# One step of a hybrid decoder trunk on one core: the order of turning x, transposed sample columns, paired logits, a 528-column gather, and the order of the tail's back-turns

## The chip, the cores and the metric

The kernel runs on one core of a Trainium2 chip. Its time is the device time of one execution in microseconds; the median of three runs is given. Work of the core is done by TensorE (PE, with its weight loads shown apart as PEld), VectorE (DVE), ScalarE (ACT), GpSimd (POOL) and SyncE (SP, which here only issues transfers). Each has its own instruction queue, and the queues meet through semaphores.

## What is computed

One layer of a decoder trunk, for 256 prompt rows and 8 sample rows that share the weights (264 tokens, `TOK`), width 2048, all in fp32. Cut to its core:

```python
xn = rmsnorm(h, norm1_g)
c_val, c_gate, l_x, l_gate = split(xn @ w_in + b_in)         # 2048 -> 4 x 1024
c  = silu(layernorm(causal_dw_conv(c_val * sigmoid(c_gate), width 31)))
r  = rg_lru(causal_dw_conv(l_x, width 4)) * gelu(l_gate)     # recurrence over tokens
h  = h + concat(c, r) @ w_out
h  = h + hier_moe(rmsnorm(h, norm2_g))                       # below
h  = h + sigmoid(rmsnorm(h, ple_norm_g) @ w_pg + b_pg) * (p @ w_ple)
y  = rmsnorm(h, final_g)
# hier_moe: the group of 4 with the largest logit, the 2 best of its 8 experts,
#   out += (silu(x @ w_gate[e]) * (x @ w_up[e])) * combine[:, e] @ w_down[e]      (512 hidden)
```

All 32 experts' weights are read, 12.6 MB each.

## The kernel before

Activations lie transposed: `hT` and the like hold 128 channels on the partitions and the 264 tokens along the free axis, in 16 blocks (`KD = 16`). A turn brings a block from rows to columns or back through PE, with the identity `ident`; it has three parts, two of 128 tokens and one of the 8 sample tokens (`ROWS`). Every engine's stream is written out by hand, in the order in which it shall run; nothing is scheduled by a tool. The stages are:

1. **x turned.** x comes by two queues and SP. DVE and ACT sum the squares of the rows, ACT takes the root, DVE makes `rb` (the factor of each token). PE turns the 16 blocks of x (`turn_x`) into four PSUM banks in turn, and ACT copies them out as `hT`; block k waits for copy k-4. After eight blocks PE turns the vectors, then `rb`, then the other eight blocks. DVE scales into `xT`.
2. **w_in**: 32 products (`dense`, 16 chunks of 264 columns in two records each), with the convolution and the recurrence beside them on DVE. The last of the old rows are turned here.
3. **w_out**: 16 products (`split_product`): each weight tile is split into two fp32r parts, the high one by ACT, the rest by DVE (`rest_weights`), and three passes are added up. After product m come the router's logits of block m-1 (`logits`, 36 columns: 4 groups and 32 experts, all in bank 7) and the turn of block m-1 back to rows (`turn_rows`), which DVE and ACT take as `h_lo` and `h_hi`. In three places the tails of the states are turned (`turn_tails`, 8 turns each).
4. **Routing.** The logits and the sum of squares are copied by DVE into `lgT`, turned on PE, and DVE picks the groups, experts and places in `NSLOT` = 528 slots (two per token). Products of `w_ple` and the rank products fill PE meanwhile.
5. **Gather.** The chosen rows are brought to their slots by products with `onehot`, in two halves of `HX` = 296 columns, 80 products each and one for the scale; DVE takes them as `xTs`. The array has 64 further columns (`WIN`) so that a window of 64 slots can start anywhere (`XW` = 592).
6. **Experts.** For each of 32 experts PE multiplies a window of 64 slots with gate and up, then down, with the two column halves of the array in use at once, and spreads the result to the tokens; POOL copies the next window. Weights come by SP as pairs of 2.1 MB (`N_PAIR` = 192, six to an expert) into six pairs of ring slots. Pair g is issued when pair g-4 (for g under 8) or g-6 has been used; pairs 8 and 9 wait for the gather. Eight units (`UNITS`) of two blocks each add an expert's result to `hT` on DVE; behind the last expert their squares are summed there.
7. **Tail.** `w_pg`: 16 products, three plain (`PG_PLAIN`) and 13 split in two by ACT and DVE. Behind product 1 PE sums the squares over the partitions with `ones`; DVE makes `rb3` from it. For each tile DVE multiplies by `rb3`, ACT takes the sigmoid, DVE multiplies with `pleT` and adds to `hT`. The table `BACK` says behind which product PE turns which finished block back to rows, into three banks that are used again and again; DVE's `take_back` multiplies it by the final gain and frees the banks. Then the last scale and the output.

`slot_loaded` counts transfers, `acc_full` finished products, `h_added` finished blocks of `hT` in stage 3, `h3_ready` in the tail, `sq3_summed` the squares of the last units, `y_taken` the taken back-turns.

Of the kernel before, what the change touches and what calls it, by code (L numbers as in the profile page):

```python
# [17 lines left out]
TOK = SEQ + NB  # L18
# [14 lines left out]
NS = 13  # L33
NS_IN = 12
# [6 lines left out]
BACK = {4: (0,), 5: (1, 2), **{m: (m - 3,) for m in range(6, KD)}}  # L41
# [9 lines left out]
HX = XW // 2  # L51
# [57 lines left out]
def build(nc, a, o):  # L109
# [80 lines left out]
    rs_bc = place("rs_bc", [P, XW], F32, r_c + 4096)  # L190
    iota = place("iota", [P, XW], F32, r_c + 6464)
    onehot = place("onehot", [P, 3, XW], F32R, r_c + 8832)
# [84 lines left out]
    posn = rt("posn", [P, 3, E])  # L277
    pm1 = rt("pm1", [P, 1])
# [21 lines left out]
    hot_zero = sem("hot_zero")  # L300
    act_order = sem("act_order")
# [49 lines left out]
    lgT_ready = sem("lgT_ready")  # L351
    logits_turned = sem("logits_turned")
# [197 lines left out]
    def _(pool):  # L550
# [49 lines left out]
        for m in range(KD):  # L600
# [66 lines left out]
    def _(pe):  # L667
        def turn(out, src, r):

            if r == P:  # L670
                return pe.transpose(out, src, ident[:, :])  # L671
            return pe.matmul(out, src, ident[:, :], start=True, stop=True)  # L672
# [40 lines left out]
        pe.wait_ge(consts_ready, 5)  # L713
        for k in range(8):
# [159 lines left out]
        for m in range(KD):  # L874
# [29 lines left out]
        pe.wait_ge(lgT_ready, 1)  # L904
        for c in range(3):
            r = ROWS[c]
            src = lgT[0:65, c * P:c * P + r]
            if r == P:
# [963 lines left out]
```

## Time and profile before

| | |
|---|---|
| median of 3 runs | 1523.83 us (1523.17 to 1524.14) |
| profiled execution | 1522.83 us |
| its span, first to last instruction | 1521.0 us |
| PE busy (products) | 1445.9 us, 95% |
| PE weight loads | 826.3 us, 54% |
| DVE, ACT, POOL busy | 631.1, 232.5, 125.7 us |
| moved by the transfers | 482.63 MB, 317 GB/s over the span |
| mean granted clock of PE | 0.984 |

The profile is of one execution, and its places are in microseconds from the first instruction. Busy shares are over the whole span, and stages differ: one stage may wait for transfers and the next for PE. The end of a PE record is modelled, and a wide fp32 product of PE leaves two records in most of the views. The granted clock is a share of the full 2.4 GHz, so 0.50 is 1.2 GHz.

### The profile page before, as it was taken

To read this page: it belongs to the slowest core of one execution; us is meant where nothing else is said; L and a number is where in the kernel's file an instruction comes from. 1 tells how busy PE (TensorE), PEld (TensorE's weight loads), DVE (VectorE), ACT (ScalarE), POOL (GpSimd) and SP (SyncE) were. 2 spreads that over 40 slices of the span, in tenths; PEclk is the share of its full clock that TensorE was granted. 3 is DMA by queue.
4 is the path that set the end of the run, shared out by engine and by line. 5 is a ranking of instruction groups with operands and counts; after the bars stand their busy time and mean duration, and the time that the engine had idled before them with its cause. 6 is when DMAs were issued, how large, how long until landed. Compare 5 with 4: busy or idle time off the path is not lost.

```text
span 1521.0 us, 17860 instructions
## 1 busy us (share of the span) xinstructions
PE 1445.9 (95%) x7481; PEld 826.3 (54%) x7481; DVE 631.1 (41%) x1245; ACT 232.5 (15%) x384; POOL 125.7 (8%) x112
## 2 busy tenths in 40 slices
PE   6999999999999999999999999999999999999896
PEld 4888887888764334333333433343343334336795
DVE  3698844654452323322322322232232223226754
ACT  4000046633300000000000000000000000004432
POOL 1000002233000000000000000000000000000331
PEclk9999999999999999999999999999999999999998
DMA  9935340354459999999999999999999999996451
GB/s 285 286 138 193 140 111 1 91 144 139 194 239 377 427 427 428 427 427 429 427 427 427 428 428 429 427 426 427 427 427 429 427 428 427 427 420 182 126 162 62
DMA packets 122203, 482.63 MB, mean 317 GB/s; under 512 B 5242, under 2 KB 87714, under 8 KB 96611
## 3 DMA queue, kind: packets, MB, share of 16 engines
q1 hardware_dynamic: 120778, 475.45, 78.7%
q0 software_dynamic: 912, 2.89, 0.7%
q10 hardware_dynamic: 432, 3.15, 0.5%
q8 instruction: 60, 0.98, 0.3%
q14 instruction: 21, 0.16, 0.0%
HBM read 479.06 MB, written 3.42 MB: 317 GB/s over the span
## 4 chain that ended last, share of the span: by engine, by line
PE 66%; DMA 26%; ACT 3%; DVE 3%; issue 1%; SPq 0%; POOL 0%; DVEq 0%; ACTq 0%; POOLq 0%
DMA ring<-in_w_up_dram 25%; PE ps L1006 22%; PE ps L696 14%; PE ps L1028 7%; PE ps L970 4%; PE ps L804 3%; PE ps L806 3%; PE ps L805 3%; PE ps L1016 2%; PE ps L1099 1%; PE ps L672 1%; PE ps L710 1%; DVE sgl L1707 1%; PE ps L671 1%; PE ps L853 1%
## 5 line engine op out<-in xcount | busy, mean ns | idle before, releaser
L1006 PE MATMUL ps<-ring,xwin 128*64 128x512 f32 x1984 | 454.0, 599 | 22.6 <-DMA ring<-in_w_up_dram 22.5
L1723 DVE TENSOR_TENSOR hT<-hT,ps 128x528 f32<-128x528 f32 x256 | 171.7, 702 | 352.4 <-PE ps L970 349.1
L1006 PEld LDWEIGHTS ps<-ring,xwin 128*64 128x64 f32 x1984 | 140.4, 137 | 285.3 <-issue 285.3
L1028 PE MATMUL ps<-ring,hid 128*64 128x512 f32 x1024 | 238.2, 620 | 0.0
L696 PE MATMUL ps<-xT,ring 128*128 128x264 f32 x1024 | 231.2, 388 | 0.0
L696 PEld LDWEIGHTS ps<-xT,ring 128*128 128x128 f32 x1024 | 195.2, 191 | 33.5
L970 PE MATMUL ps<-sel,ysb 64*128 64x264 f32 x1024 | 185.0, 415 | 1.5 <-DVE ysb L1715 0.8
L970 PEld LDWEIGHTS ps<-sel,ysb 64*128 64x128 f32 x1024 | 103.5, 186 | 111.1 <-issue 100.6
L1028 PEld LDWEIGHTS ps<-ring,hid 128*64 128x64 f32 x1024 | 73.1, 142 | 148.8 <-issue 137.7
L642 POOL COPY xwin<-xTs 128x1024 f32 x31 | 32.4, 1047 | 840.1 <-PE ps L1006 820.3
L1276 ACT ACTIVATE sgl<-ps 64x512 f32<-64x512 f32 x32 | 18.9, 589 | 524.4 <-PE ps L1006 524.4
L1354 DVE SCALAR_TENSOR_TENSOR mix<-U,vT,mix 128x256 f32<-128x256 f32 x240 | 95.3, 477 | 0.0
L1715 DVE COPY ysb<-ps 128x512 f32<-128x512 f32 x32 | 22.1, 692 | 168.4 <-PE ps L1028 168.4
L1016 PE MATMUL ps<-ident,sgl 64*128 64x64 f32 x256 | 66.4, 399 | 10.7 <-DVE sgl L1707 10.7
L1494 DVE TENSOR_TENSOR ring_r<-ring,ring_r 128x2048 fp32r<-128x2048 f32 x29 | 66.3, 2290 | 24.5 <-ACT ring_r L1181 24.3
L1016 PEld LDWEIGHTS ps<-ident,sgl 64*128 64x128 f32 x256 | 62.0, 324 | 23.7 <-DVE sgl L1707 23.7
L1279 ACT ACTIVATE ysb<-ps 128x512 f32<-128x512 f32 x32 | 19.1, 598 | 355.4 <-PE ps L1028 355.4
L1707 DVE TENSOR_TENSOR sgl<-sgl,ps 64x512 f32<-64x512 f32 x32 | 22.1, 691 | 108.6 <-ACT sgl L1276 108.5
L1181 ACT ACTIVATE ring_r<-ring 128x2048 fp32r<-128x2048 f32 x29 | 55.3, 1908 | 52.4 <-DMA ring<-in_w_out_dram 43.2
L804 PE MATMUL ps<-gx_hi,ring_r 128*128 128x264 f32 x208 | 61.3, 295 | 0.0
L804 PE MATMUL ps<-x_hi,ring_r 128*128 128x264 f32 x208 | 60.6, 291 | 0.0
L806 PE MATMUL ps<-gx_hi,ring_r 128*128 128x264 f32 x208 | 59.7, 287 | 0.0
(338 smaller groups left out, 1278.3 us busy)
## 6 DMA issues: line engine op xcount, KB each, us to landing
ring<-in_w_gate_dram SPq DMA_DIRECT2D x64, 2048.0 KB, 16.0
ring<-in_w_up_dram SPq DMA_DIRECT2D x64, 2048.0 KB, 20.5
ring<-in_w_down_dram SPq DMA_DIRECT2D x64, 2048.0 KB, 18.2
ring<-in_w_in_dram SPq DMA_DIRECT2D x32, 512.0 KB, 8.8
ring<-in_w_in_dram SPq DMA_DIRECT2D x16, 1024.0 KB, 8.1
ring<-in_w_out_dram SPq DMA_DIRECT2D x16, 1024.0 KB, 5.9
ring<-in_w_pg_dram SPq DMA_DIRECT2D x16, 1024.0 KB, 5.9
ring<-in_w_ple_dram SPq DMA_DIRECT2D x2, 1024.0 KB, 4.9
```

Source lines behind the costliest of these rows:

```text
L696: mm = pe.matmul(ps[:, n % 3, 0:TOK], w, rhs[:, k, :], start=(k == 0), stop=(k == kt - 1))
L804: pe.matmul(out, w_hi, gate_hi(t)[:, k, :], start=(i == 0), stop=False)
L805: pe.matmul(out, w_hi, gate_lo(t)[:, k, :], start=False, stop=False)
L806: mm = pe.matmul(out, w_lo, gate_hi(t)[:, k, :], start=False, stop=(i == KD - 1))
L970: mm = pe.matmul(ps[:, 4 + 2 * (u % 2) + half, 0:TOK], ysb[rows, b, i * P:(i + 1) * P], sel[rows, :], start=True, stop=True)
L1006: mm = pe.matmul(ps[part * WIN:(part + 1) * WIN, 0, :], window(k), weights(2 * j + part)[:, kk * F:(kk + 1) * F], start=(k == 0), stop=(k ...
L1016: mm = pe.matmul(ps[:, 1, t * WIN:(t + 1) * WIN], sgl[WIN:2 * WIN, :].rearrange("w (p t) -> w t p", t=4)[:, t, :], ident[WIN:2 * WIN, WIN: ...
L1028: mm = pe.matmul(ps[half * WIN:(half + 1) * WIN, 2 + b, :], hid[:, t, :], weights(8 + t)[:, q * 512:(q + 1) * 512], start=(t == 0), stop=( ...
L1181: act.activation(ring_r[:, hi_slot(t), :, :].rearrange("p k c -> p (k c)"), ring[:, lo_slot(t), :], ACT.Copy).then_inc(w_hi_ready, 1)
L1354: return dve.scalar_tensor_tensor(out=out, in0=in0, scalar=s, in1=in1, op0=op0, op1=op1)
L1494: dve.tensor_tensor(lo, ring[:, lo_slot(t), :], hi.bitcast(F32), ALU.subtract).then_inc(w_lo_ready, 1)
L1723: dve.tensor_tensor(pair, pair, ps[:, b:b + 2, 0:TOK], ALU.add).then_inc(sems["added"], 1)
```

## The change

- **Start.** PE makes 36 transpositions of the identity into a bank that is free then (`WARM`), ahead of `turn_x`. ACT squares only the 8 sample rows, DVE both blocks of 128; ACT copies turned blocks as they come, and does its square behind the fourth, the root behind the sixth.
- **Turns.** The part with 8 sample tokens was a matmul with `ident`; it is now a transposition, as the others are.
- **Logits.** Two blocks at a time, behind every second product, the even one into partitions 0 to 35 of bank 7, the odd one into 64 to 99. The sum of squares goes to bank 5. ACT copies the even logits, DVE the odd ones and the squares. `fold`, a matrix made of two pieces of the identity, adds even and odd and turns them in one product; the squares are turned by a product with one column. That is six products for three.
- **Gather.** The halves have 264 columns, no more than the 528 slots; POOL clears the 64 spare columns of `xTs`.
- **Tail.** The sum of squares comes behind product 0. DVE makes `rbt` behind the eighth rest of the activations instead of the first. A tile's step on DVE is cut in two (`gate_in`, `gate_out`) with the rest of the weights between them, a tile earlier than before. Each back-turn comes one or two products later.

```diff
+WARM = 36
-BACK = {4: (0,), 5: (1, 2), **{m: (m - 3,) for m in range(6, KD)}}
+BACK = {**{m: (m - 5,) for m in range(5, 12)}, 12: (7, 8), 13: (9, 10), 14: (11,), 15: (12,)}
-HX = XW // 2
+HX = NSLOT // 2
...
         pool.wait_ge(logits_turned, 1)
+        pool.memset(xTs[:, :, NSLOT:], 0.0).then_inc(pad_zero, 1)
...
         def turn(out, src, r):
-            if r == P:
-                return pe.transpose(out, src, ident[:, :])
-            return pe.matmul(out, src, ident[:, :], start=True, stop=True)
+            return pe.transpose(out, src, ident[:, :])
...
         pe.wait_ge(consts_ready, 5)
+        for _ in range(WARM):
+            pe.transpose(ps[:, 7, 0:P], ident[:, :], ident[:, :])
         for k in range(8):
             turn_x(k)
...
-            pe.wait_ge(h_added, m + 1)
-            mm = pe.matmul(ps[0:NG + E, 7, 0:TOK], wr[:, m, :], hT[:, m, :], start=(m == 0), stop=(m == KD - 1),
-                           skip_group_check=True)
-            return mm
+            pe.wait_ge(h_added, m + 2)
+            for part in range(2):
+                pe.matmul(ps[part * 64:part * 64 + NG + E, 7, 0:TOK], wr[:, m + part, :], hT[:, m + part, :],
+                          start=(m == 0), stop=(m == KD - 2), skip_group_check=True)
...
+            if m >= 2 and m % 2 == 0:
+                logits(m - 2)
             if m >= 1:
-                logits(m - 1)
                 turn_rows(m - 1)
...
-        logits(KD - 1)
+        logits(KD - 2)
         pe.wait_ge(sq2_summed, KD)
-        pe.matmul(ps[64:65, 7, 0:TOK], ones[:, 0:1], acc2[:, :], start=True, stop=True, skip_group_check=True)\
-            .then_inc(logits_full, 1)
+        pe.matmul(ps[0:1, 5, 0:TOK], ones[:, 0:1], acc2[:, :], start=True, stop=True).then_inc(logits_full, 1)
...
-                last = pe.transpose(ps[:, 6, c * P:c * P + 65], src, ident[0:65, 0:65])
...
+            pe.matmul(ps[0:r, 6, c * P:c * P + NG + E], lgT[:, cols], fold[:, :], start=(c == 0), stop=True,
+                      skip_group_check=True)
+            mm = pe.matmul(ps[0:r, 6, c * P + 64:c * P + 65], sqh[0:1, 0, cols], ones[0:1, 0:1], start=False, stop=True,
+                           skip_group_check=True)
...
-            if m == 1:
+            if m == 0:
                 pe.wait_ge(sq3_summed, 2 * UNITS)
...
+        def take_x(first, n):
+            for k in range(first, first + n):
+                act.wait_ge(x_turned, k + 1)
+                act.activation(hT[:, k, :], ps[:, 3 + k % 4, 0:TOK], ACT.Copy).then_inc(hT_raw, 1)
+
+        take_x(0, 4)
         act.activation(xdump[0:NB, 1, :], xrow[0:NB, 2, :], ACT.Square, accum_out=ssum[0:NB, 2:3]).then_inc(ssq_act, 1)
-        act.activation(xdump[:, 1, :], xrow[:, 1, :], ACT.Square, accum_out=ssum[:, 1:2]).then_inc(ssq_act, 1)
+        take_x(4, 2)
...
+        take_x(6, KD - 6)
...
-        dve.wait_ge(ssq_act, 2)
+        dve.wait_ge(x_loaded[1], 16)
+        link(dve.tensor_tensor_reduce(xdump[:, 0, :], xrow[:, 1, :], xrow[:, 1, :], 1.0, 0.0, ALU.mult, ALU.add, ssum[:, 1:2]))
+        dve.wait_ge(ssq_act, 1)
...
-            if i == 0:
+            if i == 7:
                 dve.wait_ge(sum3_full, 1)
...
+        for m in range(4, KD):
+            gate_in(m)
+            if m + 3 < KD:
+                rest_weights(KD + m + 3)
+            gate_out(m)
             for b in BACK.get(m, ()):
                 take_back(b)
```

The start of ACT's stream, before; `hT<-ps` are the copies of turned blocks, `xdump<-xrow` the squares:

```order
L1135 DMA xrow<-in_x_prompt_dram 128x2048
L1138 ACT_TABLE_LOAD
L1138 ACTIVATE xdump,ssum<-xrow 8x2048
L1141 ACTIVATE xdump,ssum<-xrow 128x2048
L1143 ACT_TABLE_LOAD
L1143 ACTIVATE ssum<-ssum 128x3
L1146 ACTIVATE hT<-ps 128x264 x16
```

And of the change:

```order
L1141 DMA xrow<-in_x_prompt_dram 128x2048
L1143 ACT_TABLE_LOAD
L1143 ACTIVATE ssum<-ssum 128x1
L1148 ACTIVATE hT<-ps 128x264 x4
L1151 ACTIVATE xdump,ssum<-xrow 8x2048
L1148 ACTIVATE hT<-ps 128x264 x2
L1154 ACTIVATE ssum<-ssum 128x3
L1148 ACTIVATE hT<-ps 128x264 x10
```

The copies moved ahead of the squares and the root, the square of 128 rows left ACT, and the second table load is gone.

PE's stream behind the last `w_out` product, before (`36x264` are logits, `1x264` the sum of squares, `ident,hT` a turn back to rows, `ident,lgT` the turn of the logits):

```order
L671 MATMUL ps<-ident,hT 128x128 [waits rows_lo,rows_hi,h_added]
L671 MATMUL ps<-ident,hT 128x128
L672 MATMUL ps<-ident,hT 8x128
L853 MATMUL ps<-hT,wr 36x264 [waits h_added]
L900 MATMUL ps<-acc_89,ones 1x264 [waits sq2_summed]
L671 MATMUL ps<-ident,hT 128x128 [waits rows_lo,rows_hi,h_added]
L671 MATMUL ps<-ident,hT 128x128
L672 MATMUL ps<-ident,hT 8x128
L909 MATMUL ps<-ident,lgT 128x65 [waits lgT_ready]
L909 MATMUL ps<-ident,lgT 128x65
L911 MATMUL ps<-ident,lgT 8x65
```

And of the change:

```order
L860 MATMUL ps<-hT,wr 36x264 [waits h_added]
L860 MATMUL ps<-hT,wr 36x264
L907 MATMUL ps<-acc_89,ones 1x264 [waits sq2_summed]
L676 MATMUL ps<-ident,hT 128x128 [waits rows_lo,rows_hi,h_added]
L676 MATMUL ps<-ident,hT 128x128
L676 MATMUL ps<-ident,hT 8x128
L914 MATMUL ps<-fold,lgT 128x36 [waits lgT_ready]
L916 MATMUL ps<-ones,sqh 128x1
L914 MATMUL ps<-fold,lgT 128x36
L916 MATMUL ps<-ones,sqh 128x1
L914 MATMUL ps<-fold,lgT 8x36
L916 MATMUL ps<-ones,sqh 8x1
```

The two last blocks of logits stand behind each other now, and six products take the place of three turns.

DVE's stream at the start of the tail, before (`gx_lo` the rests of the activations, `rbt` the reading of the sum, `ring_r` the rest of a weight tile, `zt<-ps` a tile's first step):

```order
L1772 TENSOR_TENSOR gx_lo<-ring,gx_hi 128x264 [waits gx_hi_ready]
L1775 TENSOR_SCALAR rbt<-ps 128x264 [waits sum3_full]
L1772 TENSOR_TENSOR gx_lo<-ring,gx_hi 128x264 [waits gx_hi_ready] x15
L1777 RECIPROCAL rb_109<-rbt 128x264 [waits root_ready]
L1494 TENSOR_TENSOR ring_r<-ring,ring_r 128x2048 [waits w_hi_ready,dve_order]
L1795 TENSOR_TENSOR zt<-ps,rb_109 128x264 [waits acc_full,fing_loaded]
L1797 TENSOR_TENSOR zt<-zt,pleT 128x264 [waits sig_ready]
L1798 TENSOR_TENSOR hT<-hT,zt 128x264 [waits dve_order]
```

And of the change:

```order
L1787 TENSOR_TENSOR gx_lo<-ring,gx_hi 128x264 [waits gx_hi_ready] x8
L1790 TENSOR_SCALAR rbt<-ps 128x264 [waits sum3_full]
L1787 TENSOR_TENSOR gx_lo<-ring,gx_hi 128x264 [waits gx_hi_ready] x8
L1792 RECIPROCAL rb_109<-rbt 128x264 [waits root_ready]
L1507 TENSOR_TENSOR ring_r<-ring,ring_r 128x2048 [waits w_hi_ready,dve_order]
L1810 TENSOR_TENSOR zt<-ps,rb_109 128x264 [waits acc_full,fing_loaded]
L1810 TENSOR_TENSOR zt<-ps,rb_109 128x264 [waits acc_full]
L1814 TENSOR_TENSOR zt<-zt,pleT 128x264 [waits sig_ready]
L1815 TENSOR_TENSOR hT<-hT,zt 128x264 [waits dve_order]
L1814 TENSOR_TENSOR zt<-zt,pleT 128x264 [waits sig_ready]
L1815 TENSOR_TENSOR hT<-hT,zt 128x264 [waits dve_order]
```

The reading of the sum moved behind eight rests, and the first steps of two tiles stand ahead of both second steps.

## Rows read from the trace of the kernel before

**Rows 1.** The page: busy time of each engine, and GB/s in 40 slices.

```profile
PE 1445.9 (95%) x7481; PEld 826.3 (54%) x7481; DVE 631.1 (41%) x1245; ACT 232.5 (15%) x384; POOL 125.7 (8%) x112
...
GB/s 285 286 138 193 140 111 1 91 144 139 194 239 377 427 427 428 427 427 429 427 427 427 428 428 429 427 426 427 427 427 429 427 428 427 427 420 182 126 162 62
```

**Rows 2.** Timeline of SP's queue, 380 to 560: start, us, the issues there.

```profile
470.68 3.76 SPq L524 DMA_DIRECT2D ring<-in_w_down_dram  x2
...
482.22 0.33 SPq L524 DMA_DIRECT2D ring<-in_w_gate_dram  x1
...
490.68 0.33 SPq L524 DMA_DIRECT2D ring<-in_w_gate_dram  x1
```

**Rows 3.** Timeline, 0 to 75: start, us, instructions in a row, idle before and its releaser.

```profile
9.75 2.29 DVE L1370 CUSTOM_DVE_ANT_0 xdump<-xrow 128x2048 f32<-128x2048 f32 x1 [8.79 <-DMA xrow<-in_x_prompt_dram]
...
10.93 1.91 ACT L1138 ACTIVATE xdump<-xrow 8x2048 f32<-8x2048 f32 x1
...
16.45 1.74 ACT L1146 ACTIVATE hT<-ps 128x264 f32<-128x264 f32 x5
...
16.87 3.35 PE L710 MATMUL ps<-ident,xrow 128*128 128x128 f32 x12 [3.81 <-ACT hT L1146]
...
21.36 0.93 PEld L728 LDWEIGHTS ps<-ident,rb 128*128 128x128 f32 x4
...
23.03 6.63 PE L710 MATMUL ps<-ident,xrow 128*128 128x128 f32 x24
...
29.59 8.59 PE L696 MATMUL ps<-xT,ring 128*128 128x264 f32 x32
...
38.84 7.29 PE L696 MATMUL ps<-xT,ring 128*128 128x264 f32 x32
```

**Rows 4.** Timeline of PE, 290 to 335.

```profile
290.38 0.64 PE L853 MATMUL ps<-hT,wr 128*36 128x264 f32 x2
...
290.94 0.44 PE L671 MATMUL ps<-ident,hT 128*128 128x128 f32 x2
...
296.38 1.94 PE L672 MATMUL ps<-ident,U 128*38 128x128 f32 x16
```

**Rows 5.** Chain that ended last, in order of time.

```profile
279.58 1.71 PE ps L824 x14
...
431.41 13.88 PE ps L1006 x64
```

**Rows 6.** Timeline of PE, 400.9 to 424.

```profile
400.97 0.34 PE L909 MATMUL ps<-ident,lgT 65*128 65x65 f32 x2 [0.50 <-DVE lgT L1574]
...
401.45 7.39 PE L696 MATMUL ps<-pT,ring 128*128 128x264 f32 x32
...
408.67 0.30 PE L924 MATMUL ps<-asg,tri 128*128 128x32 f32 x2
...
409.72 0.96 PE L927 MATMUL ps<-asg,ones 128*128 128x32 f32 x6
```

**Rows 7.** Timeline of PE, 445 to 476.

```profile
447.11 0.40 PE L951 MATMUL ps<-onehot,h_hi 128*128 128x296 f32 x1
...
458.03 0.30 PE L955 MATMUL ps<-onehot,h_smp 128*128 128x296 f32 x1
```

**Rows 8.** Timeline, 1378 to 1455.

```profile
1389.46 14.48 PE L1099 MATMUL ps<-ring 128*128 128x264 f32 x64 [0.69 <-ACT ring L1308]
...
1401.02 0.71 DVE L1766 TENSOR_TENSOR accp<-accp,sqp 128x528 f32<-128x528 f32 x1
```

**Rows 9.** Waits of PE, 1370 to 1521: us in total, times, longest us.

```profile
PE ps L671 <- DVE ring L1788: 8.2, 2, 6.3
```

**Rows 10.** The page, groups: busy us, mean ns of one, idle before and its releaser.

```profile
L1494 DVE TENSOR_TENSOR ring_r<-ring,ring_r 128x2048 fp32r<-128x2048 f32 x29 | 66.3, 2290 | 24.5 <-ACT ring_r L1181 24.3
```

**Rows 11.** Windows of 3 us: length, busy us (count) PE PEld DVE ACT POOL, PEclk, DMA, GB/s.

```profile
1437.00:1440.00 3.00, 2.92 (x12) 2.20 (x13) 1.48 (x4) 2.63 (x3) 0.01 (x1) 0.50 0.00 0
1440.00:1443.00 3.00, 3.00 (x20) 3.00 (x20) 3.00 (x5) 0.00 (x0) 2.55 (x1) 0.70 0.00 0
```

More of the change, by code:

```diff
@@ L188, in build @@
     pT = place("pT", [P, 2, TOK], F32, r_c + 20992)
-    rs_bc = place("rs_bc", [P, XW], F32, r_c + 4096)
-    iota = place("iota", [P, XW], F32, r_c + 6464)
-    onehot = place("onehot", [P, 3, XW], F32R, r_c + 8832)
+    rs_bc = place("rs_bc", [P, NSLOT], F32, r_c + 4096)
+    iota = place("iota", [P, NSLOT], F32, r_c + 6464)
+    onehot = place("onehot", [P, 3, NSLOT], F32R, r_c + 8832)
     over = place("over", [P, E, 4], F32, r_c + 18432)
@@ L277, in build @@
     posn = rt("posn", [P, 3, E])
+    fold = rt("fold", [P, NG + E])
     pm1 = rt("pm1", [P, 1])
@@ L897, in _ @@
                 last.then_inc(p_turned, 1)
-        logits(KD - 1)
+        logits(KD - 2)
         pe.wait_ge(sq2_summed, KD)
-        pe.matmul(ps[64:65, 7, 0:TOK], ones[:, 0:1], acc2[:, :], start=True, stop=True, skip_group_check=True)\
-            .then_inc(logits_full, 1)
+        pe.matmul(ps[0:1, 5, 0:TOK], ones[:, 0:1], acc2[:, :], start=True, stop=True).then_inc(logits_full, 1)
         turn_rows(KD - 1)
-        pe.wait_ge(lgT_ready, 1)
+        pe.wait_ge(lgT_ready, 2)
         for c in range(3):
             r = ROWS[c]
-            src = lgT[0:65, c * P:c * P + r]
-            if r == P:
-                last = pe.transpose(ps[:, 6, c * P:c * P + 65], src, ident[0:65, 0:65])
-            else:
-                last = pe.matmul(ps[0:r, 6, c * P:c * P + 65], src, ident[0:65, 0:65], start=True, stop=True)
-        last.then_inc(logits_turned, 1)
+            cols = slice(c * P, c * P + r)
+            pe.matmul(ps[0:r, 6, c * P:c * P + NG + E], lgT[:, cols], fold[:, :], start=(c == 0), stop=True,
+                      skip_group_check=True)
+            mm = pe.matmul(ps[0:r, 6, c * P + 64:c * P + 65], sqh[0:1, 0, cols], ones[0:1, 0:1], start=False, stop=True,
+                           skip_group_check=True)
+        mm.then_inc(logits_turned, 1)
         pe.wait_ge(pT_ready, 2)
@@ L1136, in _ @@
         act.wait_ge(ssum_set, 1)
-        act.wait_ge(x_loaded[2], 16)
+        act.activation(ssum[:, 3:4], ssum[:, 3:4], ACT.Sqrt)
+        def take_x(first, n):
[3 more added lines that the diff above has]
+        take_x(0, 4)
         act.activation(xdump[0:NB, 1, :], xrow[0:NB, 2, :], ACT.Square, accum_out=ssum[0:NB, 2:3]).then_inc(ssq_act, 1)
-        act.wait_ge(x_loaded[1], 16)
-        act.wait_ge(ssq_act, 1)
-        act.activation(xdump[:, 1, :], xrow[:, 1, :], ACT.Square, accum_out=ssum[:, 1:2]).then_inc(ssq_act, 1)
+        take_x(4, 2)
         act.wait_ge(ms_ready, 1)
         act.activation(ssum[:, 0:3], ssum[:, 0:3], ACT.Sqrt).then_inc(root_ready, 1)
-        for k in range(KD):
-            act.wait_ge(x_turned, k + 1)
-            act.activation(hT[:, k, :], ps[:, 3 + k % 4, 0:TOK], ACT.Copy).then_inc(hT_raw, 1)
+        take_x(6, KD - 6)
         act.wait_ge(consts_ready, 5)
@@ L1261, in _ @@
                 act.activation(pT[:, m - 9, :], ps[:, 5, 0:TOK], ACT.Copy).then_inc(pT_ready, 1)
+        act.wait_ge(logits_full, 1)
+        act.wait_ge(fold_ready, 1)
+        act.activation(lgT[0:NG + E, :], ps[0:NG + E, 7, 0:TOK], ACT.Copy).then_inc(lgT_ready, 1)
         rows_high(KD - 1)
@@ L1567, in _ @@
                 dve.memset(rank[:, :, :], 0.0)
-                link(dve.memset(lgT[:, :], 0.0))
+                dve.memset(lgT[:, :], 0.0)
                 dve.memset(ssum[:, :], 1.0)
+                dve.tensor_tensor(fold[:, :], ident[:, 0:NG + E], ident[:, 64:64 + NG + E], ALU.add).then_inc(fold_ready, 1)
+                dve.wait_ge(fold_ready, 1)
         dve.wait_ge(logits_full, 1)
-        dve.tensor_copy(lgT[0:NG + E, :], ps[0:NG + E, 7, 0:TOK])
-        dve.tensor_copy(lgT[64:65, :], ps[64:65, 7, 0:TOK]).then_inc(lgT_ready, 1)
+        dve.tensor_copy(lgT[64:64 + NG + E, :], ps[64:64 + NG + E, 7, 0:TOK])
+        dve.tensor_copy(sqh[0:1, 0, :], ps[0:1, 5, 0:TOK]).then_inc(lgT_ready, 1)
         rows_low(KD - 1)
@@ L1789, in take_back, with gate_in @@
                 .then_inc(y_taken, 1)
-        for m in range(KD):
+        def gate_in(m):
             dve.wait_ge(acc_full, CT_PG + m + 1)
@@ L1798, in _ @@
             dve.tensor_tensor(hT[:, m, :], hT[:, m, :], zt[:, m % 2, :], ALU.add).then_inc(h3_ready, 1)
-            if 1 <= m and m + 4 < KD:
-                rest_weights(KD + m + 4)
+        gate_in(0)
+        gate_in(1)
+        gate_out(0)
+        gate_out(1)
+        gate_in(2)
+        rest_weights(KD + 5)
+        gate_out(2)
+        gate_in(3)
+        rest_weights(KD + 6)
+        gate_out(3)
+        for m in range(4, KD):
[3 more added lines that the diff above has]
+            gate_out(m)
             for b in BACK.get(m, ()):
```

6 lines of the change are left out of this document (5 added, 1 removed).

## The prediction

> **What bounds the kernel now.** I read the page first, then the stretch before the first product, the weight queue, the chain, and the waits of PE in the tail. On the page PE is busy 95% of the span, and GB/s stands at 426 to 429 in nearly all slices from the 14th to the 35th [rows 1]. So the kernel has three parts. Up to some 480 us PE sets the pace. The expert loop is a stream of weights: 180 pairs of 2.1 MB come with and after the issue at 482.22, at 427 GB/s 884 us, and only then has the last expert its weights. The tail behind it is set by PE again. What decides whether a gain ahead of the loop reaches the end is where that stream becomes unbroken. Two pairs need 9.8 us. Those issued at 470.68 are in at 480.5, and the next issue is at 482.22: dry for 1.7 us. Those of 482.22 last to 492.0, and the issue of 490.68 finds them still at work; the later ones have more room [rows 2]. The issue of 482.22 waits for PE to free a pair in the second expert. So a microsecond that PE gains before 482 moves the whole stream by one. Gains made after 445 alone would meet the transfers after some 4 us; all that I find lies earlier, except half of the gather.
>
> **The start.** Before, ACT squares x, loads a table for the root and makes its first copy of a turned block at 16.45; PE has turned four blocks, has no bank left, and is idle until 16.87 [rows 3]. In the new order ACT takes blocks as they come: four by 13.5, the 8-row square (2.1 us with its read) to 15.5, two more blocks to 16.3, the root, then DVE's reciprocal and three multiplies to 17.5, which is when `rb` was ready before. DVE's second 128-row square is done at 14.5 (2.29 us from 12.1). PE turns eight blocks without a stop (0.83 us each, 24 in 6.63) from 9.9 to 16.5, the five vector blocks (1.2 us) to 17.7, and then does the `rb` turn that stood at 21.36. That is **3.6 us**; the rest of the stage follows in its old order. Cover: the first chunks of `w_in` must be in by 26, and they are issued by 17.
>
> The 36 extra transpositions fill the wait for x. Four wide weight loads of `rb` take 0.93 us, and a three-block group 0.83, so one costs 0.21 to 0.27 us, 36 take 7.6 to 9.9 from 2.0 us on. At 0.22 they end at 9.9, with x in at 9.7. At the dear end PE starts 2 us late and the start brings 1.6. Do they raise the clock? The first dense product takes 8.59 us against 7.29 for the next, though 6.6 us of unbroken transpositions lie right in front of it [rows 3]. So those did not bring the 2.4 GHz level; 1.3 us more means 2.6 us at 1.2 GHz. I take nothing for the clock. If the 36 raised it and it stayed, the product would lose its 1.3 us and eight blocks would go at some three quarters of 0.83: 3 us together.
> The Trainium skill says the like of the transpose mode ("TensorE: Matmul & The Clock Gate", Part 4: it does not count as busy in the same way), and the slow product agrees.
>
> **Logits two at a time.** One block costs PE 0.56 us (290.38 to 290.94) [rows 4]. The two of a pair go to different column halves of the array. In the experts' gate and up such halves run side by side: 32 products of 512 columns in 13.88 us, 0.434 each [rows 5], while one of 264 columns on the whole array takes 0.456 (16 in 7.29) [rows 3], which is 0.88 at 512. So a pair costs what one did. Blocks 0 to 13 are on PE's path, seven pairs in place of 14: 7 x 0.56 = **-3.9 us**. The last pair hides behind POOL's sum of squares, as the last two did. If the halves do not overlap, the term is 0.
>
> **Sample columns by transposition.** `L672` issues two records per turn, 16 for 8 turns in 1.94 us, where `L671` issues two for two turns [rows 4]. One record less is 0.11 to 0.12 us; a shorter pass of the one left may give up to 0.165. I take 0.13. On the path before the experts are 14 turns of rows and 24 of tails: 38 x 0.13 = **-4.9 us** (-4.3 to -6.3). In the tail 13 more: -1.7.
>
> **Logits turned by `fold`.** In place of three products (400.97 to 401.45, 0.48 us) come six in alternating shapes, twelve records. At the 0.09 us a record of the rank products (12 from 408.67 to 409.72) [rows 6] and 0.1 for each of five changes of shape that is 1.6: **+1.1 us** (0.7 to 1.7), on the path, since the routing and PE's next products both stand behind. ACT's copy runs beside DVE's two, which are as many as before.
>
> **528 columns.** The 80 products of a half stand 10.92 us apart from first to last, 0.138 each; products of 264 columns come every 0.122 (14 in 1.71) [rows 5, 7]. 80 x 0.016 = 1.3 us, with the scale records 1.35 a half: **-2.7 us**. DVE's takes follow PE one by one and shrink with it. POOL's clearing of the pad has 10 us before DVE wants the last of `onehot`.
>
> Before the stream: -3.6 - 3.9 - 4.9 + 1.1 - 2.7 = **-14.0 us**.
>
> **The tail.** First, the sum of squares moves from behind the second plain product to behind the first. DVE adds the last square at 1401.02 + 0.71 = 1401.73, while the first product ends at 1396.7 (half of 14.48 after 1389.46) [rows 8]. Before, the sum came after two products and found it done. Now PE waits from 1396.7 to 1401.8: **+5.1 us**; behind it stand products 1 and 2, whose operands are ready. Second, the back-turns. PE waits 6.3 us for DVE's take `L1788` (of 8.2 in all; the other 1.9 is at the very end and stays) [rows 9]: turn 2 needs take 0, which DVE reaches only at 1436, behind four rests of 2.29 us [rows 10], each waiting for ACT's rounding. Now turn 2 comes two products later, and DVE's rests use what ACT rounded a step earlier. A step of DVE is then 0.4 + 2.3 + 0.9 + 0.7 = 4.3 us, against 6.4 of PE: the wait goes, -6.3. With it goes what the clock took: it shows 0.50 in 1437:1440, behind the idle time, and 0.70 in the next 3 us [rows 11], so 4.8 us at half speed, -2.4. The new wait may cost the same; it is shorter, I take half, +1.2 (0 to 2.4). Tail: +5.1 + 1.2 - 6.3 - 2.4 - 1.7 = **-4.1 us**. What is late next: a rest is now due three products (19 us) after its tile's slot is free, less 2.3 for itself, which leaves 16 for load and rounding.
>
> **Sum.** The profiled execution took 1522.83 us (span 1521.0, 1.8 around it), 1.0 below the median of the runs. -18.1 gives 1504.7, or 1505.7 as a median; I say 1506.
>
> **Rivals.**
> (a) The 36 transpositions do raise the clock: 3 us more, 1503. Against it is the slow product after 6.6 us of transpositions; for it, that every third of those was narrow. 0.15.
> (b) The narrow transpositions bring nothing, as two passes in one record. Then 51 x 0.13 = 6.6 us stay: 1512.4. For it: no row shows one with 8 output rows. Against: those with 8 input rows in the start take one record. 0.12.
> The Trainium skill has a rule on this side: "TensorEngine Tiling (Array Packing)", Tile-to-Partition Mapping, Restrictions, says that column tiling disables the transpose mode for FP32 input. By it the sum would be that of (b); no run here shows it yet.
> (c) The pairs of logits run one after the other, +3.9: 1510. The experts' rows speak against it. 0.06.
> (d) The stream does not move, since its start hangs on transfers and not on PE. Then only the tail counts: 1520. The dry time before 482 speaks against it. 0.05.
> (e) The 36 cost 0.27 each: +2, 1508. 0.10.
> (f) Slower than before: each narrow transposition empties the array on both sides. A turn of rows already pays for two changes of shape, but in the tails eight narrow ones follow each other. At 0.24 us a piece, what they cost now, it is (b); each 0.01 more on 51 is 0.5 us, so at 0.46 the gain is gone, and at 0.6 it is 1531. The whole three-block group with its narrow one takes 0.83 at half clock, which speaks against such a price. 0.03.
>
> **Numbers.** Forecast 0.46, (a) to (f) as above, 0.03 for what I do not see. Its own range is 1503 to 1509. Leaving out (d), (f) and the far ends of the others: 1500.5 to 1513, the low end being (a) with the bounds of the turns. A measurement of this kernel tells 0.2% (3 us) from no change. Faster 0.93; same 0.03 (part of (d) and (f)); slower 0.04.
>
> **What would show it.** PE's idle time in 13 to 17 gone; the first dense product at 26 and still longer than the second; `hT,wr` records in twos with hardly a step between them; one record per sample turn; the issue of 482.22 at about 468; GB/s at 427 as before; in the tail a wait of 5 us for DVE's last square and none for the takes but the last 1.9. Wrong would be a stream that starts no earlier, or gaps in it.

## The result and the profile after

The changed kernel takes 1499.12 us (median of four runs, 1497.86 to 1504.21) against 1523.99 us for the kernel before on the same chips: a ratio of 0.9842, with a 95% interval of 0.9829 to 0.9856. That is 24.9 us saved where 18 were forecast, and 1.4 us below the low end of the range. The profiled execution took 1497.86 us, its span 1496.0. First the page of the changed kernel: busy time by engine, the granted clock in tenths, and GB/s, each in 40 slices.

```profile
PE 1427.9 (95%) x7469; PEld 827.5 (55%) x7469; DVE 637.2 (43%) x1248; ACT 227.0 (15%) x383; POOL 127.2 (9%) x113
...
PEclk8999999999999999999999999999999999999998
...
GB/s 270 309 155 202 122 113 1 97 172 175 191 302 412 424 428 427 429 427 427 427 428 428 427 428 429 427 426 427 428 428 428 427 428 428 427 424 189 133 173 63
```

The stream of weights is as even as before [rows 1]: it fills the same slices, from the 13th or 14th to the 36th, with one slice now 37.4 us and not 38.0. In the queue of SP (start, us, the issue) the place of [rows 2] is:

```profile
461.73 0.33 SPq L528 DMA_DIRECT2D ring<-in_w_gate_dram  x1
```

482.22 has become 461.73: 20.5 us before the stream, where 14.0 were forecast. The spans differ by 25.0, so 4.5 us came from behind it (4.1 forecast). Next PE's timeline at the start (start, us, instructions in a row, idle time before and its releaser), and the windows over it, whose last columns are granted clock, DMA share and GB/s.

```profile
2.04 7.12 PE L719 MATMUL ps<-ident 128*128 128x128 f32 x36 [2.04 <-POOL ident L560]
9.44 4.35 PE L714 MATMUL ps<-ident,xrow 128*128 128x128 f32 x24 [0.28 <-DMA xrow<-in_x_prompt_dram]
...
15.62 1.74 PE L734 MATMUL ps<-ident,rb 128*128 128x128 f32 x6 [1.10 <-DVE rb L1375]
17.29 6.63 PE L714 MATMUL ps<-ident,xrow 128*128 128x128 f32 x24
23.85 9.74 PE L700 MATMUL ps<-xT,ring 128*128 128x264 f32 x32
...
34.25 7.29 PE L700 MATMUL ps<-xT,ring 128*128 128x264 f32 x32
```

```profile
12.00:15.00 3.00, 2.52 (x16) 1.68 (x15) 2.64 (x5) 3.00 (x8) 0.00 (x0) 1.00 1.05 357
15.00:18.00 3.00, 2.38 (x9) 1.80 (x9) 1.71 (x7) 0.18 (x1) 0.00 (x0) 0.50 1.09 358
...
27.00:30.00 3.00, 3.00 (x11) 2.40 (x10) 2.11 (x9) 0.57 (x2) 3.00 (x5) 0.73 1.04 212
```

The first eight blocks of x take 4.35 us where the second eight take 6.63: PE ran at 2.4 GHz (granted 1.00) for the first, and at 1.2 GHz (0.50) from about 15.0 us, within its wait of 1.1 us for `rb` (14.5 to 15.6), to about 28.6. The turn of `rb` came 5.7 us earlier than in [rows 3]; the slower first product gave 1.15 back, and 4.6 stay.

Behind the `w_out` products (start, us, PE's instructions in a row) there are slots with logits and slots without:

```profile
289.39 0.64 PE L860 MATMUL ps<-hT,wr 128*36 128x264 f32 x4
289.96 0.55 PE L676 MATMUL ps<-ident,hT 128*128 128x128 f32 x3
...
297.07 0.49 PE L676 MATMUL ps<-ident,hT 128*128 128x128 f32 x3
297.32 0.37 PE L810 MATMUL ps<-x_hi,ring_r 128*128 128x264 f32 x1
```

A pair of logits takes 0.57 us (289.39 to 289.96), as one block did in [rows 4]. A turn of three parts by itself takes 0.25 (297.07 to 297.32) in three records. In the tail, the waits of PE from 1365 to 1500 (us in total, times, longest), and a window behind the first of them:

```profile
PE ps L1111 <- DVE accp L1781: 5.0, 1, 5.0
PE ps L676 <- DVE ring L1803: 2.5, 1, 2.5
```

```profile
1384.00:1387.00 3.00, 3.00 (x8) 2.29 (x8) 3.00 (x10) 0.33 (x2) 0.00 (x0) 0.50 0.00 0
```

The wait for the sum of squares is there with 5.0 us, as forecast, and a stretch at 1.2 GHz behind it. The wait of 6.3 us for a take [rows 9] is gone; the one at the very end is 2.5 us and was 1.9.

### The profile page after: what moved, and what is told of

Same layout as the page of the kernel before. It is cut to its first block and busy times, and to the rows that moved or that the text cites. A ratio compares the mean times of both kernels' runs of the same rounds, so it can differ in the third digit from the quotient of the medians.

```text
span 1496.0 us, 17840 instructions
## 1 busy us (share of the span) xinstructions
PE 1427.9 (95%) x7469; PEld 827.5 (55%) x7469; DVE 637.2 (43%) x1248; ACT 227.0 (15%) x383; POOL 127.2 (9%) x113
## 5 line engine op out<-in xcount | busy, mean ns | idle before, releaser
L1730 DVE COPY ysb<-ps 128x512 f32<-128x512 f32 x32 | 22.1, 692 | 166.5 <-PE ps L1034 166.5
L1722 DVE TENSOR_TENSOR sgl<-sgl,ps 64x512 f32<-64x512 f32 x32 | 22.1, 691 | 108.5 <-ACT sgl L1287 108.5
L810 PE MATMUL ps<-gx_hi,ring_r 128*128 128x264 f32 x208 | 60.2, 289 | 0.0
L811 PE MATMUL ps<-gx_lo,ring_r 128*128 128x264 f32 x208 | 59.1, 284 | 0.0
## 6 DMA issues: line engine op xcount, KB each, us to landing
ring<-in_w_up_dram SPq DMA_DIRECT2D x64, 2048.0 KB, 20.5
```

The costliest lines, as they stand in the source:

```text
L810: pe.matmul(out, w_hi, gate_hi(t)[:, k, :], start=(i == 0), stop=False)
L811: pe.matmul(out, w_hi, gate_lo(t)[:, k, :], start=False, stop=False)
```

## The experiments

Each is given by its edit to the changed kernel, the first by its edit to the kernel before. "The stage of `w_out`" is from PE's first `w_out` product to its sum of squares: 124.3 us in the kernel before, 111.7 in the changed one. "Above" and "below" compare the median with the changed kernel's 1499.12 us. The experiments ran on several chips, on which the kernel before had medians of 1523.8 to 1524.9 us, so such a difference can be off by 1 us; where it matters the ratios to the kernel before are given.

**1. Only the turns** (kernel before).

```diff
-            if r == P:
-                return pe.transpose(out, src, ident[:, :])
-            return pe.matmul(out, src, ident[:, :], start=True, stop=True)
+            return pe.transpose(out, src, ident[:, :])
```

> The kernel before with one part of the change: the 8-row turns of rows, tails and back-turns as transpositions. Theory A, that each fp32 product that stands between a transposition or an fp32r product and its neighbour costs the change of kind on both sides: a turn of three parts falls by 0.4 us (0.68 to about 0.28 behind the logits, 0.63 to 0.25 in the tail), the 24 tail turns by 0.11 each, so 14 x 0.4 + 2.75 = 8.4 us before the weight stream and 13 x 0.38 = 5 in the tail: 1510 to 1511. Rival, the prediction's own price, one record of 0.13 us less for each turn: 4.9 and 1.7, so 1517. Rival that the narrow ones bring nothing: 1524.

Measured: 1511.08 us (1509.31 to 1513.22) against 1524.89, ratio 0.9914 (0.9897 to 0.9930). The stage of `w_out` took 116.3 us, 8.1 less, where the forecast had 4.9 for the same turns. A slot with logits and turn (PE's timeline of this kernel), and the end of such a turn in the kernel before, which starts at 290.94 [rows 4]:

```profile
303.30 0.64 PE L851 MATMUL ps<-hT,wr 128*36 128x264 f32 x2
303.86 0.55 PE L670 MATMUL ps<-ident,hT 128*128 128x128 f32 x3
304.16 0.37 PE L802 MATMUL ps<-x_hi,ring_r 128*128 128x264 f32 x1
```

```profile
291.63 0.39 PE L832 MATMUL ps<-x_hi,ring_r 128*128 128x264 f32 x1
```

Logits 0.56 as before, the turn 0.30 (303.86 to 304.16), where it was 0.69 (290.94 to 291.63). So the turn's price was not that of one record. The tail became 4.4 us shorter, from 131.5 to 127.1 (first plain product to the end), though PE's waits for the takes there grew from 8.2 to 9.4 us.

**2. The turns back.** The reverse edit, in the changed kernel.

> The changed kernel with the 8-row turns as fp32 products again. Theory A: each turn of three parts gains 0.4 us again, tails 2.75 together: 14 x 0.4 + 2.75 + 5 = 13.4 us slower, 1512.5. The prediction's price: 6.6 us slower, 1505.7. If the pairs of logits are what makes the turns cheap, since half the turns no longer stand beside logits: less than 6 us slower.

Measured: 1514.12 us (1512.79 to 1515.33), 15.0 above the changed kernel (13.9 by the ratios, 0.9933 and 0.9842). The stage of `w_out` took 119.7, 8.0 more, and the tail from the first plain product to the end 130.4 in place of 127.0. Behind the wait for the sum of squares its clock was at 1.2 GHz for 3.4 us instead of 6.8, which hides 1.7 us of what its turns cost. The rest lies between the two stages, mostly in clock: from the end of the gather to the second expert it took 17.3 us and not 14.2. With experiment 1 it shows that the turns are worth 8 us before the stream, with pairs of logits or without.

**3. The steps by themselves.** 65 added products ahead of the last pair of logits, one kind behind another (the text below counts 68).

```diff
+        pe.wait_ge(pT_ready, 2)
+        probe = {
+            "T": lambda: pe.transpose(ps[:, 5, 0:P], ident[:, :], ident[:, :]),
+            "N": lambda: pe.transpose(ps[0:NB, 5, 0:P], hT[:, 0, 0:NB], ident[:, :]),
+            "M": lambda: pe.matmul(ps[0:NB, 5, 0:P], hT[:, 0, 0:NB], ident[:, :], start=True, stop=True),
+            "F": lambda: pe.matmul(ps[:, 5, 0:P], ident[:, :], ident[:, :], start=True, stop=True),
+            "L": lambda: pe.matmul(ps[0:NG + E, 5, 0:TOK], wr[:, 0, :], hT[:, 0, :], start=True, stop=True),
+            "R": lambda: pe.matmul(ps[:, 5, 0:TOK], x_hi[:, 0, 0:P], x_hi[:, 0, :], start=True, stop=True)}
+        for kind in "RRRRTTTTRRRRMRRRRNNNNMMMMNNNNTTTTFFFFTTTTRRRRFFFFRRRRLLTTTTLLRRRR":
+            probe[kind]()
```

> The changed kernel with a row of 68 added products ahead of the last pair of logits, into a bank that is free, of six kinds (fp32r of 264 columns, transposition of 128, transposition with 8 output rows, fp32 product with 8 output rows, fp32 product 128 x 128, fp32 logits), in fours behind each other, to read each step from start to start. Theory A: an fp32 product costs two records and about 0.2 us at each of its borders (0.1 over the step that it would else take), a transposition of any width one record of 0.11 and nothing extra beside fp32r or another transposition. So M alone between fp32r products takes some 0.4 us, N alone some 0.11. Rival: the borders cost by the number of output rows, so N beside T or R shows extra time too.

Measured in a single run: the timeline of PE; L912 is R, L907 T, L909 M, L908 N, L910 F.

```profile
380.88 0.73 PE L912 MATMUL ps<-x_hi 128*128 128x264 f32 x4
381.45 0.60 PE L907 MATMUL ps<-ident 128*128 128x128 f32 x4
381.80 0.73 PE L912 MATMUL ps<-x_hi 128*128 128x264 f32 x4
382.46 0.39 PE L909 MATMUL ps<-ident,hT 128*8 128x128 f32 x2
382.77 0.76 PE L912 MATMUL ps<-x_hi 128*128 128x264 f32 x4
...
384.87 0.60 PE L908 MATMUL ps<-ident,hT 128*8 128x128 f32 x4
385.31 0.60 PE L907 MATMUL ps<-ident 128*128 128x128 f32 x4
385.74 1.06 PE L910 MATMUL ps<-ident 128*128 128x128 f32 x8
386.64 0.60 PE L907 MATMUL ps<-ident 128*128 128x128 f32 x4
```

Read by starts: R4 with T4 takes 0.92 us (380.88 to 381.80), which is 4 x 0.12 + 4 x 0.11. R4 with one M takes 0.97 (381.80 to 382.77), so M takes 0.49 where a transposition takes 0.11: two records of 0.11 and 0.27 at its two borders. Four N take 0.44 (384.87 to 385.31), no more than four T. Four F, the fp32 product of full width, take 0.90 (385.74 to 386.64) for eight records, without a border. So theory A held for M and fell for F: what costs is an fp32 product with few output rows (8 or the 36 of the logits), about 0.1 to 0.14 us on each side, and not every fp32 product. Why it costs that was not tried. The rival fell too: a transposition with 8 output rows has no border.

**4. Logits one at a time.**

```diff
-            pe.wait_ge(h_added, m + 2)
-            for part in range(2):
-                pe.matmul(ps[part * 64:part * 64 + NG + E, 7, 0:TOK], wr[:, m + part, :], hT[:, m + part, :],
-                          start=(m == 0), stop=(m == KD - 2), skip_group_check=True)
+            pe.wait_ge(h_added, m + 1)
+            part = m % 2
+            pe.matmul(ps[part * 64:part * 64 + NG + E, 7, 0:TOK], wr[:, m, :], hT[:, m, :],
+                      start=(m < 2), stop=(m >= KD - 2), skip_group_check=True)
...
-            if m >= 2 and m % 2 == 0:
-                logits(m - 2)
             if m >= 1:
+                logits(m - 1)
                 turn_rows(m - 1)
...
-        logits(KD - 2)
+        logits(KD - 1)
```

> The changed kernel with the logits one block at a time again, still into the two column halves and with the turn by fold. The prediction's term: 7 x 0.56 = 3.9 us slower. Theory A adds the borders: a slot with logits and turn takes 0.87 us, two of them 1.74 against 0.25 + 0.88 = 1.13 now, 0.1 more for the product behind: 7 x 0.7 = 4.9 us slower, 1504. If the halves do not overlap: no difference.

Measured: 1506.08 us (1504.73 to 1509.06), 7.0 above. The stage of `w_out` took 116.3 us, 4.5 more: seven blocks of 0.56 us are 3.9, and the other 0.6 I put down to spared borders. The other 2.5 us lie outside that stage. In the profile it is clock: from the end of the gather to the second expert 17.4 us and not 14.2 (experiment 7 shows how much such stretches can be).

**5. The sum of squares behind the second product.**

```diff
-            if m == 0:
+            if m == 1:
                 pe.wait_ge(sq3_summed, 2 * UNITS)
```

> The changed kernel with the sum of squares behind the second plain product again, as in the kernel before. Theory: the wait of 5.0 us for the last accp goes, and with it the stretch of 6.8 us at 1.2 GHz that follows it (3.4 us at most): 5 to 8.4 us faster, 1491 to 1494. Rival: the wait only moves, since DVE or ACT (rbt, root, the first rests) are late for the split products, and the time stays at 1499.

Measured: 1491.88 us (1489.18 to 1494.77), 7.2 below the changed kernel; ratio to the kernel before 0.9788 (0.9769 to 0.9808). By its median it is the fastest version of this study. Its timeline and one window:

```profile
1369.85 14.48 PE L1105 MATMUL ps<-ring 128*128 128x264 f32 x64 [0.68 <-ACT ring L1319]
1384.16 1.05 PE L1111 MATMUL ps<-accp,ones 128*128 128x264 f32 x4
```

```profile
1384.00:1387.00 3.00, 3.00 (x15) 2.58 (x14) 3.00 (x9) 0.00 (x0) 0.00 (x0) 1.00 0.42 118
```

PE goes from product to sum without a wait, and the clock stays at 1.00 there. From the first plain product to the first split one it takes 22.1 us, in the changed kernel 30.2. So the one moved line cost the change 5.0 us of waiting and 3.1 of clock, for which the forecast had put 1.2.

**6. BACK of before.**

```diff
-BACK = {**{m: (m - 5,) for m in range(5, 12)}, 12: (7, 8), 13: (9, 10), 14: (11,), 15: (12,)}
+BACK = {4: (0,), 5: (1, 2), **{m: (m - 3,) for m in range(6, KD)}}
```

> The changed kernel with the table BACK of before, in PE's and DVE's order. If the later back-turns are what took the wait of 6.3 us away: it is back, 1502 to 1508. If the new order of DVE's steps (the rests a tile earlier) did: no difference, since turn 2 finds its bank taken, or up to 1 us faster, for less is left behind the last product.

Measured: 1499.17 us (1496.55 to 1501.92), no difference. PE's waits in its tail:

```profile
PE ps L676 <- DVE ring L1803: 2.7, 2, 2.5
```

The wait of 6.3 us stays away with the old table, so the later back-turns are not needed for that. That DVE's new order (the rests a tile earlier, between a tile's two steps) took it away alone is not shown. This kernel, too, waits 5.0 us for the sum of squares and loses clock behind it, so PE begins its split products 7.7 us later after the tail's start than before, and 7.7 is more than 6.3. In experiment 5 PE is not late, and the wait stays away as well, but with the new table. The old table with the sum behind the second product was not run.

**7. No transpositions at the start.** `WARM = 0`.

> The changed kernel without the 36 transpositions. If they raise the clock: the first eight blocks take 6.6 us and not 4.35, the turn of rb stands at about 17.8 and not 15.6, the first dense product starts at 26 and not 23.85, the second at 34.8 to 36.3, and the whole is 0.5 to 2.5 us slower (1499.6 to 1501.6). If the chip raises the clock without them as soon as x is there: no difference, the eight blocks at 4.4 us. If they bring the whole 5.7 us by which the first dense product came earlier: 5.7 us slower.

Measured: 1500.44 us (1498.51 to 1506.86), not to be told from the changed kernel: 1.3 above by the medians, while the ratio to the kernel before is 0.9836 and the changed kernel's 0.9842. The timeline:

```profile
9.25 6.60 PE L714 MATMUL ps<-ident,xrow 128*128 128x128 f32 x24 [9.25 <-DMA xrow<-in_x_prompt_dram]
...
16.99 1.74 PE L734 MATMUL ps<-ident,rb 128*128 128x128 f32 x6
...
25.22 10.00 PE L700 MATMUL ps<-xT,ring 128*128 128x264 f32 x32
```

The eight blocks are slow again, and the second dense product starts at 35.88, 1.6 us later than with the 36. The column of the granted clock does not show that the blocks are slow. Here is the same window of this kernel and, below it, of the one with 18 transpositions (experiment 10), both at the slow pace:

```profile
12.00:15.00 3.00, 3.00 (x13) 1.61 (x11) 1.91 (x3) 2.57 (x5) 0.00 (x0) 1.00 1.08 365
12.00:15.00 3.00, 3.00 (x12) 1.73 (x12) 2.31 (x4) 2.40 (x3) 0.00 (x0) 0.50 1.06 361
```

The traces have their first record of the clock at 30.5 us here, at 32.1 in the kernel before and at 8.2 in the changed one, and ahead of it the column reads 1.00 even where PE idles. Up to there the level has to be read from PE's pace.

The profiled execution, 1506.9 us, also shows the clock at 0.50 in three later stretches, near 257, near 390 and from 447 to 457 (a window around the third, same columns):

```profile
446.00:458.00 12.00, 12.00 (x34) 6.14 (x36) 1.75 (x4) 1.56 (x4) 1.96 (x2) 0.57 0.90 384
```

From the third dense product to the second expert this kernel and the changed one run the same instructions. They took 410.5 us in the profiles of the changed kernel and of experiments 5, 6, 9, 10 and 11, 412.2 in that of 8, and 416.7 in those of 7 and 12. Such stretches, whose place and number differ between profiles over the same instructions, move a run by up to 6.3 us. The three values are those of one, two and three stretches at 1.2 GHz, 3.4, 6.8 and 17.1 us of it in all.

**8. Ten transpositions in the wait for rb.**

```diff
         last.then_inc(vec_turned, 1)
+        for _ in range(10):
+            pe.transpose(ps[:, 1, 0:P], ident[:, :], ident[:, :])
```

> The changed kernel with ten more transpositions of the identity in the 1.1 us in which PE waits for rb, after the vector blocks. Theory, that the granted clock fell at 15 us because PE idled there: it stays at 1.0, the eight later blocks take 4.4 us and not 6.6, the first dense product 7.3 and not 9.7: up to 4.6 us faster, 1494.5. Rival, that transpositions hold no clock for long, so that it falls at 15 us with or without the idle time: no difference, 1499.

Measured: 1501.25 us (1497.82 to 1506.71), no gain. In its profile the clock fell at 12.4 us already, with PE at work since 9.5 (before that it had idled for 1.6 us, waiting for x), and was back at 19.2. So the fall does not simply follow the wait for `rb`, and neither theory holds. The first dense product took 7.4 us, and then PE waited 2.0 us for the old rows.

**9. Two blocks ahead of rb.**

```diff
         last.then_inc(vec_turned, 1)
+        for k in range(8, 10):
+            turn_x(k)
 
         pe.wait_ge(rb_ready, 1)
...
-        for k in range(8, KD):
+        for k in range(10, KD):
             turn_x(k)
```

> The changed kernel with two of the eight later blocks of x turned ahead of the turn of rb. Both theories of the clock give the 1.1 us of waiting that useful work takes: 1498. If the clock stays up with it, as in the run with ten idle transpositions, 4.6 us more: 1493.5. Rival: the two blocks wait for ACT's copies and push the turn of rb back: 1499 or later.

Measured: 1502.36 us (1497.16 to 1509.56), no gain, though the clock stayed at 1.00 until 30.7 us and the first dense product began 4 us earlier:

```profile
19.88 5.61 PE L700 MATMUL ps<-xT,ring 128*128 128x264 f32 x24
26.08 2.05 PE L700 MATMUL ps<-xT,ring 128*128 128x264 f32 x8 [0.60 <-DMA ring<-in_w_in_dram]
30.92 0.46 PE L750 MATMUL ps<-ident,stage 120*128 120x120 f32 x1 [2.79 <-DMA lstage<-in_state_lru_conv_dram]
...
32.57 8.06 PE L700 MATMUL ps<-xT,ring 128*128 128x264 f32 x32
```

PE waits for a chunk of `w_in` and then for the old rows, which come in the same queue. The third dense product starts at 41.98 against 42.89: of 4 us 0.9 are left. So an earlier start of the first dense product meets the transfers next.

**10 and 11. 18 transpositions, and 18 fp32 products, in place of 36 transpositions.**

> The changed kernel with 18 transpositions of the identity instead of 36, so that PE idles from about 6 us until x is there at 9.4. If the clock follows unbroken work, it isn't raised by then: eight blocks in 6.6 us, as without any. If 18 are enough and the clock outlasts the idle time: eight blocks in 4.4 us.

> The changed kernel with 18 fp32 products of the identity by itself (two records each, 36 in all) instead of 36 transpositions. If transpositions and products count alike for the clock: the granted clock rises at 7 to 8 us as with the 36 and eight blocks take 4.4 us. If products count for more, it rises earlier or stays up over the wait for rb, and the first dense product is faster than 9.7 us.

Measured, in a single run each: 1498.71 and 1498.03 us. The starts of the two timelines:

```profile
2.04 3.74 PE L719 MATMUL ps<-ident 128*128 128x128 f32 x18 [2.04 <-POOL ident L560]
9.61 6.63 PE L714 MATMUL ps<-ident,xrow 128*128 128x128 f32 x24 [3.82 <-DMA xrow<-in_x_prompt_dram]
```

```profile
2.05 7.06 PE L719 MATMUL ps<-ident 128*128 128x128 f32 x36 [2.05 <-POOL ident L560]
9.80 4.36 PE L714 MATMUL ps<-ident,xrow 128*128 128x128 f32 x24 [0.70 <-DMA xrow<-in_x_prompt_dram]
```

With 18 transpositions PE idles for 3.8 us and the blocks are slow; with 36 records of either kind they are fast. Transpositions raised the clock as fp32 products did. The 18 had done it too: the starts of the transpositions stand 0.21 us apart up to 5.3 us and 0.11 behind, and the clock was at 0.50 again from 8.7 us, with PE idle since 5.8. With the 36 of the changed kernel the same step in pace comes at about 8 us (6 records in 7:8, 10 in 8:9).

**12. Experiments 5 and 9 together.**

> The changed kernel with both: two later blocks of x ahead of rb, and the sum of squares behind the second plain product. If the gains add up, 1491.9 less 1 (clock as before) or less 5.7 (clock stays up): 1490.8 or 1486.

Measured: 1492.91 us (1486.12 to 1496.24), not to be told from experiment 5 alone. The lowest run lies where both gains together were expected (1486); it was not profiled. The profiled one lost 6.2 us to the clock before the second expert.

## Why the prediction was wrong

Against the profiled execution before, in us. The last column names what shows it.

| term | forecast | measured | |
|---|---|---|---|
| start | -3.6 | -4.6 | second dense product 38.84 to 34.25 |
| logits in pairs | -3.9 | -4.5 | experiment 4 |
| 38 turns before the experts | -4.9 | -8.1 | experiments 1 to 3 |
| turn by `fold` | +1.1 | +1.1 | 400.97 to 401.45; now 383.56 to 385.14 |
| 528 columns | -2.7 | -2.5 | the halves with their scale 12.6 and 12.8, now 11.4 and 11.5 |
| clock and rest before 482 | 0 | -1.9 | below |
| before the stream | -14.0 | -20.5 | 482.22 to 461.73 |
| tail | -4.1 | -4.5 | the rest of the 25.0 |

**The step that failed** is "Sample columns by transposition": "One record less is 0.11 to 0.12 us; a shorter pass of the one left may give up to 0.165. I take 0.13." For the tails of the states it was right: a narrow turn fell from two records of 0.11 us to one, 2.7 us for the 24. For the turns of rows it was not: each fell by some 0.4 us, 0.49 for the fp32 product against 0.11 for the transposition (experiment 3). I had read 1.94 us for 16 records [rows 4], where eight such products follow each other and the borders are paid once, and carried it to places where one stands alone. The rows to read were the starts around a single turn. That is 3.2 us more before the stream and 3.3 more in the tail, of the 6.9 by which 25.0 exceeds the forecast of 18.1; the rest is the clock before the stream and smaller terms that partly cancel. Rival (f) even said that such a turn "already pays for two changes of shape", and took it for granted that the transposition would go on paying. The Trainium skill's rule cited for rival (b) ("TensorEngine Tiling (Array Packing)", Tile-to-Partition Mapping, Restrictions) did not show here: three records for a turn of three parts, and 0.44 us for four narrow ones, are no two passes.

**In the tail** the forecast of 4.1 us came near the measured 4.5 by luck, since errors cancelled. The 13 turns brought 5.0 us and not 1.7. One of them by its starts, in the kernel before and then in the changed one:

```profile
1423.50 0.38 PE L671 MATMUL ps<-ident,hT 128*128 128x128 f32 x2
...
1424.12 0.39 PE L804 MATMUL ps<-gx_hi,ring_r 128*128 128x264 f32 x1
```

```profile
1417.05 0.49 PE L676 MATMUL ps<-ident,hT 128*128 128x128 f32 x3
1417.29 0.37 PE L810 MATMUL ps<-gx_hi,ring_r 128*128 128x264 f32 x1
```

That is 0.62 and 0.24. The sum of squares cost 8.1 (22.1 us from the first plain product to the first split one, now 30.2), 5.0 by the wait as forecast and 3.1 by the clock where I had taken 1.2, half of the bound. At the very end up to 1.7 us were lost that were not in the sum: the last wait for a take grew by 0.6, and the stretch at 1.2 GHz in which the kernel ends from 11.0 to 13.3 us, which is 1.1 at most. The wait of 6.3 us for the take went as forecast; but "now turn 2 comes two products later" was not needed for it, and PE's own delay of 7.7 us may have hidden it (experiment 6).

**The start**: rival (a) was right about the clock and not about its worth. The 36 did raise the clock, in spite of the first dense product's slowness in [rows 3], which I had read as proof that transpositions do not. What that row shows is only that PE was slow at 29.6; it came to full pace at about 32 in that profile, after PE had been at work since 16.9. The Trainium skill's sentence on the transpose mode ("TensorE: Matmul & The Clock Gate", Part 4), which I set beside it, did not hold here: eight blocks took 4.35 us behind the 36 transpositions and 6.60 without them (experiment 7), and experiments 10 and 11 show no difference to products. With the higher clock the turn of `rb` stood at 15.6, without it at 17.0. But the clock fell before it was of use for the dense product, and what it could give there the transfers of `w_in` would take (experiment 9). By themselves the 36 are worth 1.6 us at the second dense product (34.25 against 35.88), where (a) had 3, and no difference that the run times can tell. Without them the start brings 3.0 us (38.84 to 35.88), where the forecast had 3.6.

**The clock before the stream** was not in the sum. Before, PE ran at 1.2 GHz for 6.8 us behind the gather; in the changed kernel's profile for 3.4 us. The stretches, windows of the kernel before and then of the changed one:

```profile
464.00:467.00 3.00, 3.00 (x9) 1.05 (x9) 1.33 (x3) 0.78 (x2) 0.00 (x0) 0.50 1.02 437
467.00:470.00 3.00, 3.00 (x12) 0.80 (x10) 0.00 (x0) 0.00 (x0) 0.00 (x0) 0.67 0.89 377
```

```profile
444.00:447.00 3.00, 3.00 (x10) 1.06 (x11) 1.33 (x3) 1.17 (x3) 0.00 (x0) 0.68 1.01 431
447.00:450.00 3.00, 3.00 (x14) 0.94 (x12) 0.00 (x0) 0.00 (x0) 0.00 (x0) 0.75 1.02 437
```

From the end of the gather to the second expert that is 1.7 us. Since such stretches come and go between profiles over the same instructions (experiment 7), I count it as no gain of the change.

**What was right**: that the stream moves as one piece (from the second expert to the tail 915.6 us before and after), the overlap of the logits' halves, the gather, `fold`, and the new wait of 5 us.

## What to carry to other kernels

Price a small instruction by the starts of its neighbours at the very place where it stands, and not by the mean of a row of its like: what it costs can be its borders. A single narrow fp32 product between products of another kind cost more than four times a transposition that does the same. When an operation is moved ahead of a wait, look at what its input needs; one such line here cost 7 to 8 us.

## What the runs showed of the hardware

- An fp32 product with 8 or 36 output rows has a border of 0.1 to 0.14 us on each side, beside transpositions and fp32r products alike; a full-width fp32 product and a transposition with 8 output rows have none.
- 36 transpositions brought PE to 2.4 GHz before 9.4 us, as 18 fp32 products of two records did: eight blocks in 4.35 and 4.36 us, 6.60 without. 18 transpositions raised it at 5.3 us, and 3.8 us of idling left PE at 1.2 GHz for the next blocks. When it falls again was not settled: it fell at 15.0 us within a wait of 1.1, at 12.4 with PE at work (experiment 8), and in experiment 9 not before 30.7, within a wait of 2.8.
- The column of the granted clock reads 1.00 up to the first record of the clock in the trace (32.1 us in the kernel before, 30.5 in experiment 7), also where PE's pace is that of 1.2 GHz.
- The same instructions from the third dense product to the second expert took 410.5, 412.2 and 416.7 us, with one, two and three stretches at 1.2 GHz in them. A difference of a few us between single runs of such kernels is no evidence.
